# MLP up products in three groups of 352 columns in the first half and two of 512 in the second, in place of four each

## The reference: what is computed

```python
x = x + gate_m * rmsnorm(mix, g_post_mix)              # mix = the mixer's output projection

h = rmsnorm(x, g_pre_ffn) * (1 + scale_f) + shift_f    # (2048 + 32) x 1024
y = jnp.square(jax.nn.relu(h @ w_up)) @ w_down         # w_up 1024 x 4096, w_down 4096 x 1024
x = x + gate_f * rmsnorm(y, g_post_ffn)
```

## Time and profile before

| | us |
|---|---|
| median of 3 runs (3108.83, 3108.84, 3113.99) | 3108.84 |
| the profiled execution | 3114.03 |
| its span, first to last instruction | 3112.3 |
| TensorE busy (89% of the span) | 2766.7 |
| VectorE busy (48%) | 1481.7 |
| ScalarE busy (28%) | 867.4 |
| GpSimd busy (10%) | 307.3 |

### The profile page before, as it was taken

How to read it: one execution, slowest core, us unless ns; L and a number is a source line. 1 busy time by engine, 2 the same in 40 slices (tenths; PEclk the granted TensorE clock), 3 DMA queues, 4 the chain that set the end, 5 groups by cost and what they waited for, 6 DMA issues and landing times. The chain is left out here.

```text
span 3112.3 us, 45866 instructions
## 1 busy us (share of the span) xinstructions
PE 2766.7 (89%) x18510; PEld 2421.8 (78%) x18510; DVE 1481.7 (48%) x2020; ACT 867.4 (28%) x1632; POOL 307.3 (10%) x417
## 2 busy tenths in 40 slices
PE   4999999975748768699799999999988999999996
PEld 2998989973426556588689889898878989988995
DVE  2646464725556555345444444444454444344444
ACT  2434343322334314233322112121123112211211
POOL 1111111110001111111100000000005000000003
PEclk6999999996869768699899999999999999999998
DMA  6554545434237334445421101011034101110113
GB/s 216 155 161 153 153 144 150 149 100 149 58 94 207 106 111 118 133 146 178 128 83 54 52 29 54 27 54 54 27 95 153 55 27 54 54 52 29 54 54 108
DMA packets 354373, 309.39 MB, mean 99 GB/s; under 512 B 41970, under 2 KB 308511, under 8 KB 354232
## 3 DMA queue, kind: packets, MB, share of 16 engines
q1 hardware_dynamic: 341208, 263.86, 29.0%
q0 software_dynamic: 13040, 43.81, 4.1%
HBM read 235.86 MB, written 72.70 MB: 99 GB/s over the span
## 5 line engine op out<-in xcount | busy, mean ns | idle before, releaser
L81 PE MATMUL up_ps<-h_hi,w_up_hi 128*128 128x264 f32 (+1 forms) x2048 | 580.3, 283 | 19.8 <-DVE h_lo L2762 12.4
L82 PE MATMUL up_ps<-h_lo,w_up_hi 128*128 128x264 f32 (+1 forms) x2048 | 583.3, 285 | 0.0
L83 PE MATMUL up_ps<-h_hi,w_up_lo 128*128 128x264 f32 (+1 forms) x2048 | 580.6, 283 | 0.0
L2784 DVE TENSOR_TENSOR y<-y,down_ps 128x1024 f32<-128x1024 f32 (+1 forms) x272 | 332.1, 1221 | 315.8 <-PE down_ps L83 315.3
L81 PE MATMUL down_ps<-w_down_hi,u_hi 128*128 128x512 f32 x1088 | 433.4, 398 | 18.2 <-issue 9.7
L83 PE MATMUL down_ps<-w_down_hi,u_lo 128*128 128x512 f32 x1088 | 429.7, 395 | 0.0
L82 PE MATMUL down_ps<-w_down_lo,u_hi 128*128 128x512 f32 x1088 | 427.7, 393 | 0.0
L81 PE MATMUL proj_ps<-h_hi,w_in_hi 128*128 128x262 f32 x1408 | 407.3, 289 | 16.7 <-DVE h_lo L656 13.5
L81 PEld LDWEIGHTS up_ps<-h_hi,w_up_hi 128*128 128x128 f32 x2048 | 389.3, 190 | 22.6 <-issue 13.8
L82 PE MATMUL proj_ps<-h_lo,w_in_hi 128*128 128x262 f32 x1408 | 402.5, 286 | 0.0
L83 PE MATMUL proj_ps<-h_hi,w_in_lo 128*128 128x262 f32 x1408 | 402.1, 286 | 0.0
(11 more groups left out here) (490 smaller groups left out, 3765.2 us busy)
## 6 DMA issues: line engine op xcount, KB each, us to landing
w_in_raw<-in_w_in SPq DMA_DIRECT2D x88, 512.0 KB
w_up_raw<-in_w_up SPq DMA_DIRECT2D x66, 512.0 KB
w_down_raw<-in_w_down SPq DMA_DIRECT2D x64, 512.0 KB, 4.7
proj_scratch<-chunk_out POOLq DMA_DIRECT2D x88, 256.0 KB, 3.6
w_ada_cols<-in_w_ada SPq DMA_DIRECT2D x8, 2048.0 KB, 9.2
qkv<-proj_scratch SPq DMA_DIRECT2D x16, 768.0 KB, 6.0
p_w_ada_cols<-in_w_ada SPq DMA_DIRECT2D x4, 2048.0 KB, 15.2
prep_qk<-proj_scratch SPq DMA_DIRECT2D x16, 512.0 KB, 4.3
```

The source lines that it names most:

```text
L81: nc.tensor.matmul(out, whi, mhi, start=first, stop=False)
L82: nc.tensor.matmul(out, whi, mlo, start=False, stop=False)
L83: return nc.tensor.matmul(out, wlo, mhi, start=False, stop=last)
L2784: v.tensor_tensor(acc, acc, pd[r, (par * H.tiles + t) % 2], ALU.add).then_inc(H.s_y, 1)
```

## The change

The number of groups becomes an attribute of the half, `groups`: 3 in the first half (352 columns each), 2 in the second (512 each). It replaces Q in the width of a group, in the loops over j and in every count of the semaphores `up_summed` and `relu_done`. The PSUM tile keeps its four banks (QM = 4), of which three and two are now used. Per chunk the up product takes 3 * 24 = 72 matmuls in place of 96 in the first half, and 2 * 24 = 48 in place of 96 in the second; the number of columns streamed stays the same. ScalarE does 3 and 2 relu copies per chunk in place of 4. The attribute `last`, which nothing reads, goes.

```diff
@@ Half.__init__
-        self.last = 1 if half == 0 else 0
+        self.groups = 3 if half == 0 else 2
@@ mlp
-        Q = 4
+        QM = 4
...
-        pu = m.ps("up_ps", [P, Q, 512])
+        pu = m.ps("up_ps", [P, QM, 512])
@@ TensorE
                 for H in halves:
-                    qn = H.n // Q
+                    Q, qn = H.groups, H.n // H.groups
...
-                    def up(G, par, H=H):
+                    def up(G, par, H=H, Q=Q):
...
                                 if H is second:
-                                    pe.wait_ge(first.s_re, 2 * NG * Q + Q)
+                                    pe.wait_ge(first.s_re, (2 * NG + 1) * first.groups)
@@ ScalarE
                 for H in halves:
-                    act.sem_inc(H.s_re, Q)
+                    act.sem_inc(H.s_re, H.groups)
...
-                    qn = H.n // Q
-
-                    def up(G, par, H=H, qn=qn):
+                    Q, qn = H.groups, H.n // H.groups
+
+                    def up(G, par, H=H, qn=qn, Q=Q):
@@ VectorE
-                            dve.wait_ge(H.s_re, f * Q + 2 * Q)
+                            dve.wait_ge(H.s_re, f * H.groups + 2 * H.groups)
```

## The result

The changed kernel takes 3102.39 us (median of 20 runs), the kernel before 3110.22 (20 runs). The ratio is 0.9973, with a 95% interval of 0.9967 to 0.9979: 8.4 us less, between 6.5 and 10.3. The forecast was 16.4 us less. The direction and the places are right, the size is twice too large. The median lies inside the stated range (3084 to 3104) and outside the forecast's own band (3086 to 3096).

The account below looks back on a forecast made before the run. The prediction took TensorE's matmul stream as the bound. It summed 5.2 us saved in the first half and 14.8 in the second, less 3.6 for relu tails, to 16.4 us less: 3108.8 to 3092.4 us, range 3084 to 3104.

Parts of the forecast that it names:

- What bounds the kernel: Long MLP stretches: TensorE's matmul stream is the limit; each up matmul costs 11.5 to 12.1 ns over its columns.
- Rival 2: Up products: excess grows with columns, not per instruction; only tails remain, 3.6 us more, 3112.4; chance 0.03.
- rival 3: Up products: weight loads hold up narrow matmuls, wide ones cost columns alone; 65 us less, 3043; chance 0.05, or part.
- the Trainium skill's rule: Matmul gap of N / 2.4 + 2.5 ns; by it alone the up products save 5.5 us in place of 20.0.
- The cost of a wide matmul: Up products: 227.3 ns for 512 columns (14.0 over), 159.7 for 352 (13.0 over); bounds 11.5 to 17.4 over.
- rival 1: Wide up matmuls cost a down matmul's 17.4 ns over: 512 alone 3097.3 us, chance 0.20; 352 too 3107.2, chance 0.09.
- 352 columns: First-half up product: 13.0 ns over the columns, 159.7 ns a matmul, saving 5.2 us over 248 kk.
- The tail: Each chunk's last, wider relu delays the third down tile: 1.1 us first half, 2.5 second, 3.6 us more together.
- The end: GpSimd's residual adds of down(15) end last; that chain moves with TensorE and keeps its length.
- Chunk 0 and the change of halves: No saving in first-half chunk 0 or second-half up(0); the idle before up(1) grows from 7.6 to 8.6 us.
- No wait comes from it: Up stages: with two groups, relu and ScalarE's other work finish before TensorE returns to a bank, so nothing waits.
- Rival 4: Up stages: wide matmuls take 173.7 (352) and 240 ns (512); 33 us more, 3142; chance 0.05, or part.

Follow-up runs that it names:

- packed_second: The changed kernel with the second half's rows of h and u 1024 floats apart in place of 1056: 3089.1 us, ratio 0.9926 to the kernel before.
- packed_h_shifted: The changed kernel with the second half's h rows 1024 floats apart but begun 128 bytes into their tiles, u unchanged: 3102.72 us, 0.9971 to the kernel before.
- the reordering: The changed kernel with VectorE making the second chunk's u_lo after the down stage's first add, at most changes from up to down: 3096.6 us, 0.9949 to before.
- packed_four: Four groups in both halves as in the kernel before, with the second half's rows of h and u 1024 floats apart: 3109.78 us, 0.9997 to before.
- combined_1088: The changed kernel with second-half h and u rows 1024 floats apart, first-half u rows 1088, and second chunk's u_lo after the first add: 3075.16 us, 0.9882 to before.

## Why the forecast was twice too large

- **What bounds the kernel, and that fewer matmuls pay per instruction: right.** TensorE stayed the bound, and with packed rows the excess is 13.3 ns a matmul at 256 and at 512 columns. Rival 2, an excess by column, and rival 3, a weight load that holds up narrow matmuls, both fall with that. The size in the Trainium skill's rule ("TensorE: Matmul & The Clock Gate", section "Back-to-back issue gap") doesn't hold here either: its 2.5 ns stand against 13.3 in the evenest stages measured. The prediction left out that the page gives this rule for the isolated matmul, and says that a stream of weight loads and matmuls, which this kernel is, keeps another spacing.
- **The cost of a wide matmul: the step that failed.** The prediction took 14.0 ns over for 512 columns, since "the up product is built like the output projection (one bank for 24 matmuls)". Measured is 18.6. The likeness that counts is not the bank but where the rows lie: with the same banks and packed rows the up product stands at the output projection's 226.7 ns (packed_second), and with the packed rows moved by 128 bytes it is back at 232.3 (packed_h_shifted). The down stage shares the 1056-float rows, stood at 17.4, and was the nearer row. At 240 kk x 6 matmuls x 4.7 ns this is 6.8 us of the 8 that are missing. This was the first case of rival 1 in kind (512 columns cost what a down matmul costs), with 18.6 in place of 17.4, and it had been given a chance of 0.20. The prediction's own sign of being wrong was a matmul of over 232 ns; the measured one sits on that mark.
- **352 columns: right within its size.** 13.4 ns over in place of 13.0: 248 x 9 x 0.4 = 0.9 us.
- **The tail: right.** Forecast 1.1 + 2.5 = 3.6 us. Measured 15 x (25.18 - 25.12) + 15 x (22.34 - 22.15) = 0.9 + 2.8 = 3.7.
- **The sum with the measured prices.** First half 248 x (1458 - 9 x 160.1) = 4.2 us. Second half 240 x (1426 - 6 x 232.0) = 8.2. Less 3.7 is 8.7 us; the MLP became 8.2 us shorter. The 14 up stages of each half that stand alone, and the downs after an up, give 8.1 us of it. That the rest adds up to nearly nothing is luck: the change of halves is 1.6 us shorter, the start 0.3 us longer, and the last down stage 1.3 us longer (the next two points).
- **The end: "keeps its length" was wrong.** The last down stage, down(15) of the second half, takes 25.87 us from its first matmul to its last before and 27.16 after, with the same instructions. TensorE idles 3.85 us just before it in both kernels. The granted clock then stands at the lower of its two levels (1.2 GHz) for a stretch, and a matmul takes 427 ns in place of 227: five full distances before, eleven after. The windows view around that start, before and then after (clock 0.83 and 0.66):

```profile
3060.00:3070.00 10.00, 6.16 (x22) 4.68 (x21) 4.71 (x4) 2.00 (x3) 0.00 (x0) 0.83 0.30 105
```

```profile
3045.00:3055.00 10.00, 6.15 (x16) 4.60 (x15) 3.49 (x3) 1.99 (x2) 0.00 (x0) 0.66 0.31 105
```

  This stage takes 26.9 to 27.2 us in three of the nine kernels and 25.9 to 26.2 in the other six. There is one profiled execution of each, so no run shows whether the change causes it.
- **Chunk 0 and the change of halves: right that nothing is gained at chunk 0, wrong in a number at the change.** From the first up matmul to the first down stage it is 58.8 us before and 59.0 after. The wait before up(1) of the second half did not grow from 7.59 to 8.6 us. Its row in after:

```profile
2373.78 0.29 PEld L81 LDWEIGHTS up_ps<-h_hi,w_up_hi 128*128 128x128 f32 x1 [6.54 <-ACT relu L2702]
```

In the experiments with two groups in the second half it was 6.3 to 7.7 us. From the start of up(0) to that of up(1) it is 30.4 us before and 28.8 after, and 28.6 to 30.4 in the other kernels. Why the load chain was quicker in this execution was not tested. "No wait comes from it" was slightly wrong too: with two groups TensorE idles 0.55 us between the two chunks of that up(0), which the wait before up(1) hides, since the load chain ends it and not up(0).
- **Rival 4, slower**, needed 17.8 ns over at both widths. It was true at 512 and far from it at 352.

## What to carry to other kernels

A wider matmul saved its full fixed price, 13.3 ns an instruction here, only where its operands were read evenly: look at the single distances in the trace, not only at their mean, and treat a pattern that goes on while the other engines are idle as a matter of addresses. Take the price of a shape that isn't in the trace from a stage whose operand rows lie in the same way, rather than from one that fills its banks in the same way. Packing and padding the rows cost no instruction here and, on top of the two groups and together with the reordering, brought three times what the change of groups did. With four groups packing alone brought nothing that the runs can tell from no change (0.9997, 0.9988 to 1.0007), so the two changes have to be tried together.

## What the runs showed of the hardware

- With h and u in rows 4096 bytes apart from the start of their tiles, the distance between float32 matmuls was constant: 120.0 ns for 256 columns (packed_four), 226.7 for 512 (packed_second), which is 13.3 ns over one column a cycle at 2.4 GHz. With rows 4224 bytes apart, or all rows shifted by 128 bytes, 512 columns took 232.0 to 232.3 ns on average with single steps up to 241. For 256 columns the uneven rows were a little quicker, 118.8. Why they help the narrow matmul and hurt the wide one was not settled.
- The place of the rows counts for both operands. In the up stages h is the moving data and the weights' rows were never changed; in the down stages u is the weights and the moving rows were never changed. That multiples of 256 bytes are enough was shown for the weights alone (4352 bytes, combined_1088).
- After a wait of a fraction of a microsecond, the second matmul follows the first after 0.34 us in place of 0.23, so a short stall costs 0.11 us more than its length. The following few distances are uneven too, 228 to 236 ns in packed_second, 0.03 us in all. The rows of the changed kernel:

```profile
2716.54 0.50 PE L81 MATMUL down_ps<-w_down_hi,u_hi 128*128 128x512 f32 x1
...
2716.88 0.40 PE L82 MATMUL down_ps<-w_down_lo,u_hi 128*128 128x512 f32 x1
```
